# Layer B of a two-block attention kernel: key tiles begin 64 tokens before the query tiles, two key chunks a step, four bias buffers, and the turns of the probabilities inside the projected unit

## What is computed

```python
def mixer_b(hn, w_in, w_out, q_gain, k_gain, rpb):
    proj = hn @ w_in
    q, k, v, gate = jnp.split(proj, 4, axis=-1)
    q = rms_norm(q.reshape(b, s, N_HEADS, HEAD_DIM), q_gain) * (HEAD_DIM ** -0.5)
    k = rms_norm(k.reshape(b, s, N_HEADS, HEAD_DIM), k_gain)
    ...
    cstart = np.clip(qcol - NA_COLS // 2, 0, GRID_W - NA_COLS)
    ...
    col_valid = jnp.asarray((kc >= cstart[..., None]) & (kc < cstart[..., None] + NA_COLS))
    ...
        logits = jnp.einsum('bhcqd,bhrcjd->bhcqrj', qr, kr).astype(jnp.float32) + bias
        logits = jnp.where(col_valid[:, :, None, :], logits, NEG_INF)
        p = jax.nn.softmax(logits.reshape(b, N_HEADS, n_cb, NA_COL_BLOCK, wr * NA_SLAB), axis=-1)
        out = jnp.einsum('bhcqrj,bhrcjd->bhcqd', p, vr)
    ...
    y = y * jax.nn.silu(gate)
    return y @ w_out
```

## Time and profile before

| | |
|---|---|
| median of 3 runs | 1702.52 us (1697.07 to 1703.32) |
| the profiled execution | 1699.86 us, its span 1698.1 us |
| TensorE matmul busy in the span | 1578.5 us (93%) |
| VectorE, ScalarE, GpSimd busy | 813.7, 766.4, 784.5 us |
| mean granted TensorE clock | 0.969 of full speed |

### The profile page before, as it was taken

One profiled execution on the slowest core, in us unless ns is written; L12 is line 12 of the kernel. 1 busy time (PEld: TensorE's weight loads), 2 busy tenths in 40 slices (PEclk: granted clock), 3 DMA queues, 4 the chain that ended last, 5 costly groups with the idle time before them and its releaser, 6 DMA issues. The chain is left out here.

```text
span 1698.1 us, 30316 instructions
## 1 busy us (share of the span) xinstructions
PE 1578.5 (93%) x12050; PEld 1288.7 (76%) x12050; DVE 813.7 (48%) x1662; ACT 766.4 (45%) x1407; POOL 784.5 (46%) x472
## 2 busy tenths in 40 slices
PE   7899999999999998889999988999978898899997
PEld 4788888888888886667777766676757886688876
DVE  4224342433434345345655434279536764575535
ACT  4535536363544534346556643245664343232222
POOL 4734425262534433364455543425647651365651
PEclk8999999999999999999999998999988999799999
DMA  7413232231323230354544203432000000333331
GB/s 172 120 56 97 74 92 87 66 113 53 112 69 98 64 89 1 94 140 138 152 126 141 79 28 87 117 77 75 26 27 3 3 4 15 87 99 97 89 89 60
DMA packets 247188, 136.60 MB, mean 80 GB/s; under 512 B 24390, under 2 KB 241518, under 8 KB 246999
## 3 DMA queue, kind: packets, MB, share of 16 engines
q1 hardware_dynamic: 220824, 109.19, 23.5%
q10 hardware_dynamic: 26224, 25.47, 5.3%
HBM read 132.11 MB, written 2.52 MB: 79 GB/s over the span
## 5 line engine op out<-in xcount | busy, mean ns | idle before, releaser
L318 PE MATMUL a_proj<-h_low,w_high 128*128 128x512 f32 x472 | 190.1, 403 | 1.5 <-POOL h_low L931 0.8
L912 POOL TENSOR_TENSOR a_sq_low<-a_sq,a_sq_high 128x512 fp32r<-128x512 f32 x48 | 62.0, 1291 | 279.1 <-ACT a_sq_high L764 279.1
L892 POOL TENSOR_TENSOR w_low<-a_w_raw,w_high 128x1024 fp32r<-128x1024 f32 x64 | 158.3, 2474 | 66.3 <-ACT w_high L731 66.3
L320 PE MATMUL a_proj<-h_high,w_high 128*128 128x512 f32 x472 | 185.7, 393 | 0.0
L319 PE MATMUL a_proj<-h_high,w_low 128*128 128x512 f32 x472 | 184.6, 391 | 0.0
L892 POOL TENSOR_TENSOR w_low<-b_w_raw,w_high 128x1024 fp32r<-128x1024 f32 x40 | 103.3, 2584 | 101.0 <-ACT w_high L731 101.0
L318 PE MATMUL b_proj<-h_low,w_high 128*128 128x512 f32 x288 | 116.4, 404 | 1.4 <-POOL h_low L931 0.8
L320 PE MATMUL b_proj<-h_high,w_high 128*128 128x512 f32 x288 | 113.3, 394 | 0.0
L319 PE MATMUL b_proj<-h_high,w_low 128*128 128x512 f32 x288 | 112.8, 392 | 0.0
L812 ACT ACTIVATE a_pt<-a_turned 128x512 f32<-128x512 f32 x64 | 37.8, 591 | 154.2 <-PE a_turned L610 154.2
L318 PEld LDWEIGHTS a_proj<-h_low,w_high 128*128 128x128 f32 x472 | 88.8, 188 | 23.1 <-DVE a_qk L962 3.2
(11 more groups left out here) (451 smaller groups left out, 4306.0 us busy)
## 6 DMA issues: line engine op xcount, KB each, us to landing
a_w_raw<-in_a_w_in_dram SPq DMA_DIRECT2D x78, 512.0 KB, 3.7
b_w_raw<-in_b_w_in_dram SPq DMA_DIRECT2D x30, 512.0 KB, 4.2
b_ada_w<-in_ada_w_dram ACTq DMA_DIRECT2D x24, 512.0 KB, 3.6
f_wt<-in_w_in_dram SPq DMA_DIRECT2D x22, 512.0 KB, 3.8
a_bias<-scr_a ACTq DMA_DIRECT2D x16, 576.0 KB, 4.7
sparse_w_raw<-in_w_in_dram SPq DMA_DIRECT2D x17, 512.0 KB, 3.8
a_w_raw<-in_a_w_out_dram SPq DMA_DIRECT2D x8, 512.0 KB, 3.7
b_w_raw<-in_b_w_out_dram SPq DMA_DIRECT2D x8, 512.0 KB, 3.9
```

The costliest lines, as they stand in the source:

```text
L318: nc.tensor.matmul(out, lh, rl, start=first, stop=False)
L320: return nc.tensor.matmul(out, lh, rh, start=False, stop=last)
L892: nc.gpsimd.tensor_tensor(low(slot_of(b)), raw[:, n % RAW, :, :], high(slot_of(b)), ALU.subtract).then_inc(s_wl, 1)
L912: nc.gpsimd.tensor_tensor(sql[:, :], sq[:, u % 2, :], sqh[:, :], ALU.subtract).then_inc(s_sql, 1)
```

## The change

- Key tiles begin 64 tokens ahead of the query tiles. Query tile r now sees tokens 128r - 64 to 128r + 191, which is 256 keys in all four. In tiles 0 and 3 the range leaves the sequence on one side by 64 tokens; there the scores of those 64 columns are made from the 64 tokens at the other end of the sequence, and the mask shuts them out. Scores are one product of 256 keys a head in steps 1 and 2, and one of 64 and one of 192 in steps 0 and 3.
- v's tiles are shifted likewise: the first of the four holds the last 64 and the first 64 tokens and is made by two products with the identity, the other three by transposes. Step r uses tiles r and r + 1 (mod 4).
- Bias and mask are 256 wide for every tile, three additions of 256 a head (one was 384).
- There are four bias and four raw bias buffers (`L.bias_heads`). The load for the head four later is issued in step 0 (`L.bias_at`), it was step 3 for the head three later. After the units of pair p, GpSimd masks heads 2p+2 and 2p+3; it was 2p+1 and 2p+2.
- The turns of step t-1's probabilities stand inside the projected unit, behind the fifth of its eight pieces (`half_way`). In the last pair, and in the step behind it, they stand ahead of the small products, and in step 0 behind unit 4.

Layer A's tables get the values they had (three buffers, step 3).

```diff
-B_SEGS = (256, 384, 256)
+B_SEGS = (256, 256, 256)
...
-    for blk, k0, n in ((0, 0, 256), (1, 0, 384), (3, 256, 256)):
+    for blk, k0, n in ((0, -HD, 256), (1, HD, 256), (3, 5 * HD, 256)):
...
-            def project(p, u):
+            def project(p, u, half_way=None):
...
                         if p == 0 and (u, k) in L.squares_at:
                             sum_squares(0, L.squares_at.index((u, k)))
+                        if k == KT // 2 and half_way:
+                            half_way()
                 elif L.turn_v:
                     pe.wait_ge(s_pf, UNITS * p + NQK + 2)
-                    for c in range(4):
-                        mm = nc.tensor.transpose(out[:, c * P:(c + 1) * P], vfm[:, c * P:(c + 1) * P], T.ident)
+                    for half, k0 in ((0, SEQ - HD), (1, 0)):
+                        nc.tensor.matmul(out[half * HD:(half + 1) * HD, 0:P], vfm[:, k0:k0 + HD], T.ident, start=True, stop=True)
+                    for c in range(1, 4):
+                        mm = nc.tensor.transpose(out[:, c * P:(c + 1) * P], vfm[:, c * P - HD:c * P + HD], T.ident)
...
-                    if t:
+
+                    def turns():
                         turn(t - 1, 0)
                         turn(t - 1, 1)
                     if p and r == 0 and t < STEPS:
                         project(p, UNITS - 1)
                     if p < PAIRS - 1:
-                        project(p + 1, r)
-                    elif t < STEPS:
+                        project(p + 1, r, turns if t else None)
+                    else:
+                        turns()
+                    if p == PAIRS - 1 and t < STEPS:
...
-                if r == ROWS - 1 and 2 * p + h + BH < HEADS:
-                    load_bias(2 * p + h + BH)
+                if r == L.bias_at and 2 * p + h + L.bias_heads < HEADS:
+                    load_bias(2 * p + h + L.bias_heads)
...
-                    for head in (2 * p + 1, 2 * p + 2):
+                    for head in (2 * p + 2, 2 * p + 3):
...
-    L.bias_cols, L.raw_cols, L.max_cols = B_MASK, 384, 384
-    spans = [(0, 256), (0, 384), (P, 384), (256, 256)]
-    seg0 = [0, 256, 256, 640]
-    L.score_plan = [[(h, h, n * P, 0, k0 + n * P, P, n == w // P - 1) for n in range(w // P) for h in range(2)]
-                    for k0, w in spans]
...
+    L.bias_cols, L.raw_cols, L.max_cols = B_MASK, 256, 256
+    L.bias_heads, L.bias_at = 4, 0
+    seg0 = [0, 256, 256, 512]
+
+    def pieces(r):
+
+        lo = r * P - HD
+        return [(SEQ - HD, 0, HD), (0, HD, 192)] if r == 0 else [(lo, 0, 192), (0, 192, HD)] if r == 3 else [(lo, 0, 256)]
...
+    L.chunks = [[(r, 0), ((r + 1) % 4, 0)] for r in range(4)]
+    L.mask_plan = [(c0, 256, 0, c0) for c0 in (0, 256, 512)]
```

## The result

The changed kernel took 1740.64 us (median of 4, 1738.27 to 1742.92) beside 1701.43 us for the kernel before (1697.07 to 1703.32). The ratio is 1.0237 with a 95% interval of 1.0219 to 1.0254: slower, +39.2 us. Its profiled span is 1739.3 us against 1698.1, with a mean granted clock of 0.960 against 0.969.

A forecast was written before the change was run, and what follows sets the result against it. It took TensorE's own work plus a little waiting as the bound. Per pair 33.40 - 1.34 - 1.0 + 4.7 + 0.85 + 0.75 + 2.05 = 39.4; six pairs +36.0, total +36, 1738.5 us, range 1717 to 1750.

The forecast's parts named there:

- The case: Whole kernel: the moved turns delay ScalarE and VectorE, so TensorE waits and its clock falls; +36 us, 1738.5, chance 0.64.
- a long wait for the v copy in step 0: TensorE, layer B, step 0: waits 4.7 us for VectorE's v copy in place of 1.34; 3.5 in the last pair.
- The gate: VectorE, step 3: the gate begins 6.9 us behind the step's start, where it is 2.81 today.
- Waits for banks: TensorE's projection in steps 2 and 3: waits of 0.85 and 0.75 us for banks freed late by VectorE's takes.
- Clock: TensorE behind the long wait: 4.1 us at half speed, losing 2.05 us a pair (bounds 0 and 3).
- TensorE's work: TensorE, each pair: fewer score, turn and v records, dearer turning of v; together -1.0 us (to -1.25).
- First pair: First pair of layer B: two bank waits but no long one, first step without turns; +0.3 us.
- Last pair: Last pair of layer B: a 3.5 us wait and 2.05 of clock, against the old wait, clock and work; about -0.3 us.
- Clock stays up: TensorE behind the long wait: the wait comes without a clock fall; +23 us, 1725, chance 0.12.
- Chain absorbed: Start of step 0: VectorE or ScalarE finish before TensorE asks; -12 to -21 us, about 1686, chance 0.10 (partial absorption 0.05 more).
- Masks as the limiter: VectorE behind GpSimd's masks: the 27.5 us of waits pass to TensorE, so removal gains; about +16, 1718, chance 0.03.
- Turns dear inside an accumulation: TensorE's projected unit: turns there cost up to 0.18 us extra on each side; +10 us, 1748, chance 0.06.

The follow-up runs named there:

- e8: Changed kernel with both engines' copies of the turned probabilities moved behind what they delay, and VectorE's modulation product at its step's end: 1700.19 us, ratio 1.0011.
- e4: Changed kernel with VectorE's modulation product moved from ahead of the v copy to the step's end: 1730.61 us; ratio 1.0178 without one outlying execution.
- e3: Changed kernel with 18 extra unread matmuls (12 in the last pair) on TensorE ahead of the turn of v in step 0: 1724.19 us, ratio 1.0139.
- e1: Changed kernel with the turns of the probabilities back directly behind the scores, the rest kept: 1695.49 us, 0.9971 of the kernel before.
- e7: e1 with three bias buffers, loaded in step 3 as before: 1697.60 us, 0.9993 of the kernel before.
- e2: Kernel before with only the turns moved into the projected unit: 1751.36 us, ratio 1.0303.
- e5: Changed kernel with ScalarE's copy of the turned probabilities behind exps and norm, VectorE's behind inversions and takes: 1723.65 us, ratio 1.0139.
- e10: Kernel before with only VectorE's modulation product moved to the end of its step: 1698.45 us, ratio 0.9991.
- e9: e6 with the turns inside the projected unit in step 0 alone: 1684.49 us, 0.9914 of the kernel before.
- e6: e1 with VectorE's modulation product moved to the end of its step: 1682.73 us, 0.9920 of the kernel before.

## Why the prediction was right, and where its terms were off

**The case** was the forecast one, and its largest term held: a long wait for the v copy in step 0. I predicted 4.7 us in six pairs and 3.5 in the last, and measured 4.77 and 3.14. The gate was to begin 6.9 us behind the scores and began at 6.92. The reason for it, each engine's program with the copies in front, is shown by e8 (order changed, turns left) and e4 (end of the chain). Behind the gate, though, two errors cancelled. From the gate to the end of the v copy I took the 6.70 us of the kernel before, and it was 6.75; but the gate's first operation took 0.41 in place of 0.79, and the modulation product 1.71 in place of 1.28. By the rows of the last section both go by what GpSimd runs at that moment. The walk left that out, so this part is luck.

**Waits for banks**: 0.85 and 0.75 predicted, 0.76 and 0.70 measured.

**Clock**: 2.05 us a pair predicted. Against the 7.39 us of e3 the six pairs lost 1.35, 2.20, 2.68, 1.33, 2.19 and 2.66, mean 2.07. e3 shows it as a term of its own. The mean was right by more luck than method: I had the same loss in each pair, and it depends on something that shifts from pair to pair in a cycle of three.

**TensorE's work**: the term was mis-sized, -1.0 predicted, -0.77 measured. At full clock e1's pair has 33.13 - 1.84 = 31.29 us of work against 33.40 - 1.34 = 32.06. The turn of v took more: from its start to the next unit it is 0.67 us (816.62 to 817.29 in e1) against 0.36 (816.17 to 816.53 in the kernel before), 0.31 more where I had 0.115. That is most of the difference. (The old wait of 1.34 us, which I gave as seven times, came six times; the sum uses it six times.)

**First pair**: +0.3 predicted, +1.1 measured; the two waits less the saved work are 1.46 - 0.77 = +0.7. The remaining 0.4 I did not trace.

**Last pair**: the worst term, -0.3 predicted, +3.8 measured. The wait came, but I gave the clock 4.1 us at half there too. It stood at 0.50 from about 1025.1 to 1038.8, some 13.7 us, where before it was 3.4: (13.7 - 3.4) / 2 = 5.1 more, less 1.0 of work. TensorE's work there is sparse, with products one column wide. That alone doesn't explain it: with nearly the same work the clock was back after 3.4 us in the kernel before and in e7 (wait of 1.91), and after 10 to 17 us in e2, e4, e5, e8 and e10. What decides between the two is open.

For the six pairs together: long wait less the old one, 6 x 3.43 = 20.6; banks 6 x 1.46 = 8.8; clock 12.4; work -4.6. The sum is 37.2 of 38.5 measured; the other 1.3, some 0.2 a pair, I did not find.

**The rivals.** Clock stays up: refuted in each pair, and e3 prices it at 16 us, beside my 14 for seven pairs (36 less 14 is +22; I wrote +23 and 1725). Chain absorbed: refuted; e8 shows what it would have taken, a reordering of two other engines. Masks as the limiter: refuted, the wait went from 27.5 to 0.9 us without a gain in the six pairs, and e7 puts it back for about 2 us by the medians (3.5 in its last pair). Turns dear inside an accumulation: refuted. From 832.12 the turns take 0.35 and the projection matmul behind them 0.31 in place of 0.23, 0.43 in all, where the turns had 0.46 before. e9 and e8 say the same with whole pairs.

## What to carry to other kernels

When work that feeds other engines is moved later in one engine's program, look at what those engines' programs have queued behind the operation that takes its result, and follow it to the next wait of the bottleneck engine. Here 0.46 us of turns a step, which cost nothing extra at their new place, made each pair some 6 us longer (39.8 against 33.9 in e1), and moving their consumers and the modulation product too took it back. A wait also costs what the clock loses behind it: filling the wait with products that nobody reads was worth 16 us.

## What the hardware showed that I had not expected

**VectorE held up beside GpSimd.** The same operation on the same shape took very different times. In each case an operation of GpSimd was under way when it began, a subtraction (`w_low`) or, in the changed kernel, a mask addition. Two more pairs of timeline rows; VectorE in e10:

```profile
811.47 2.73 DVE L1074 SCALAR_TENSOR_TENSOR b_ada_sum<-b_ada_w,b_cact,b_ada_sum 128x1024 f32<-128x1024 f32 x1
```

GpSimd in e10:

```profile
810.75 2.36 POOL L892 TENSOR_TENSOR w_low<-b_w_raw,w_high 128x1024 fp32r<-128x1024 f32 x1 [4.40 <-ACT w_high L731]
```

VectorE in e6:

```profile
811.65 2.57 DVE L1078 SCALAR_TENSOR_TENSOR b_ada_sum<-b_ada_w,b_cact,b_ada_sum 128x1024 f32<-128x1024 f32 x1
```

GpSimd in e6:

```profile
810.78 2.36 POOL L896 TENSOR_TENSOR w_low<-b_w_raw,w_high 128x1024 fp32r<-128x1024 f32 x1 [4.23 <-ACT w_high L735]
```

The timeline of GpSimd in the changed kernel shows the mask addition beside the product that began at 823.26 there:

```profile
823.16 0.72 POOL L908 TENSOR_TENSOR b_bias<-b_raw_bias,b_band 128x256 f32<-128x256 f32 x1
```

The modulation product alone takes 1.28 us, the gate's first operation 0.41. Add what GpSimd's operation still has to run at VectorE's start:

| operation, kernel | left of GpSimd's | + own time | measured |
|---|---|---|---|
| product, e5 | 2.31 | 3.59 | 3.40 |
| product, e10 | 1.64 | 2.92 | 2.73 |
| product, e6 | 1.49 | 2.77 | 2.57 |
| product, changed kernel | 0.62 | 1.90 | 1.71 |
| gate, e1 | 0.90 | 1.31 | 1.19 |

The sum is right to 0.2 us each time, and always above. So VectorE waits for GpSimd's operation to end rather than running slower beside it. The Trainium skill says this in "SBUF — State Buffer", section "Who interferes with whom": the two share a port pair, which a VectorE instruction needs when it has two inputs in SBUF or runs in a two-port mode; it is an exclusive lock, and whoever issues first keeps it for the whole instruction while the other is blocked. The rows agree. No run here took GpSimd's operation away, so that it is the cause is read from these rows, not shown by an experiment.

**A short wait can halve the clock.** In the six pairs, the granted clock stayed at 1.00 behind waits of 1.34 us, 0.97 (e6) and 0.81 (e9); behind 1.84 us it fell to the lower level of 1.2 GHz for a stretch in three pairs of six in e1, and in four of six in e7. A wait near 1.8 us is therefore worth more than its length to remove, and e6 over e1 is the case: the six pairs took 193.2 us in place of 203.25, 10 less, of which 5.5 are waiting (11.0 us of waits against 5.5) and 4.5 the clock's three falls at 1.5 each. The ratios, 0.9920 and 0.9971, say some 9 us.
